# Two streams or two equal halves: how layer one's 768 tokens are cut into two matmul ranges

## The chip, the cores and the metric

The kernel runs on one core of a Trainium2 chip. The metric is the time of one execution in device microseconds (us). The kernel before took 2801.38 us, the median of three runs (2800.25 to 2804.05).

## The reference, cut to what matters

Two layers of a transformer with parallel branches run over two streams: 512 latent tokens `x` and 256 context tokens `ctx`, both 1024 wide. In each layer the input is normalised and modulated and then projected; grouped-query attention, differential attention and a convolution branch work side by side, are merged with gates, and a SwiGLU feed-forward follows. All of it is in 32-bit floats.

```python
for l in range(DEPTH):                       # DEPTH = 2
    last = l == DEPTH - 1
    h  = modulate(rms_norm(x,  g_norm1[l]), sh1,  sc1)
    hc = modulate(rms_norm(xc, g_norm1[l]), csh1, csc1)
    gq, gk, gv, dq, dk, dv, cu       = project_heads(h  @ w_in[l], *qk_gains, rope)
    gqc, gkc, gvc, dqc, dkc, dvc, cuc = project_heads(hc @ w_in[l], *qk_gains, None)
    # latent queries attend to [context keys ; latent keys], context queries to context keys
    y = merge_branches(h, o_gqa, o_diff, cu, lam_init, *branch_w)
    x = x + gt1 * y
    x = x + gt2 * swiglu(modulate(rms_norm(x, g_norm2[l]), sh2, sc2), w_ffn_in[l], w_ffn_out[l])
    if not last:
        ...                                  # the same for xc, with its own modulation
return x
```

Layer one (index 0 in the code) therefore works on all 768 tokens. In layer two (index 1) the context is only needed for keys and values, and all else works on the 512 latent tokens.

## The kernel before, in words

Activations lie transposed in SBUF, features on the 128 partitions and tokens along the free axis: columns 0 to 511 are the latent tokens, 512 to 767 the context. `H` (normalised input) and `RB` (branch results, or in attention the tiles `QB`, `KB`, `VB`, `PT`) hold each value as a high and a low part. Weights come as tiles of 128 output features by up to 1024 inputs, that is up to eight chunks of 128x128. A tile's way is: DMA from SP into one of two `STG` buffers, high part by ScalarE (ACT, L748, `hi`), low part by GpSimd (POOL, L390, `split`) into one of three slots of `WHI` and `WLO`, then TensorE (PE). `product` (L467) issues three matmuls a chunk (L469, L470, L471): high by high, high by low, low by high.

`ranges(l, wide)` (L204) says into which column ranges the tokens are cut, since one PSUM bank takes at most 512 columns. Everything that projects takes its ranges from it. `tile` (L477) runs through all chunks for the first range into one of the two banks `acc0` and `acc1`, and then through all chunks again for the second range into the other bank. With `ready`, each chunk of the first range waits until its moving data is there (after a norm, at the start of a branch, of the output projection and of the feed-forward's second half). `between` puts a small piece of other PE work into the middle of the second range (`turn_mod`, L535, the transposes of a row of the modulation, or the sums of head norms).

In attention (`attention` on PE, L607) the order is written out. A head has six items of 128 queries in layer one: four of latent queries with 768 keys and two of context queries with 256 keys. PE does for each item the transposes of the probabilities (`turn_probs`, L587), the scores of the next item (`scores`, L574), a portion of the next head's projections (`slot(j, 2*i)`), the weighted sum (`weigh`, L593), and a second portion. `FILL` (L37) gives the size of each of the twelve portions in chunks of three matmuls: `[3, 3, 2, 3, 3, 2, 3, 3, 2, 3, 2, 3]` for a grouped-query head (tiles q and a, two ranges each, 32 chunks) and `[8, 4, 4, 8, 4, 4, 8, 4, 4, 8, 4, 4]` for a differential one (k, q, v, g, 64 chunks). In both a first range ends with its third or first portion and the second range with the third after it or the next two. All projections within attention go to bank `acc0` (`tile_chunks`, L497), so a range can start only when ACT has emptied the range before: `evac_norm` (L769, one Identity into `XG`, one Square into `XS`), `evac_copy` (L795) or `evac_conv_a` (L804). These stand in ACT's own written-out order behind the softmax work of the item. DVE reduces, divides and combines the probabilities (L1169, L1189, L1202).

A range that crosses column 512 holds tokens of both streams. `stream_pieces` (L123) cuts it, and the residual (L1315), `evac_conv_a` and the convolution's splits issue one instruction a piece.

Of the kernel before, what the change touches and what calls it, by code (L numbers as in the profile page):

```python
# [30 lines left out]
LAT, CTX = 512, 256  # L31
# [98 lines left out]
def build(nc, xT, vecs, consts, wdw, w_mod, w_in, w_gate, w_br, w_out, w_fi, w_fo, out):  # L130
    x_next = nc.dram_tensor("x_next", (P, KC, LAT), F32).ap()

    with ExitStack() as ctx:
# [69 lines left out]

        def ranges(l, wide):  # L204
            if l == 0:
                return [(0, 384), (384, 384)]
            return [(0, LAT), (LAT, CTX)] if wide else [(0, LAT)]

        def blocks(l):
# [6 lines left out]
        def halves(n):  # L216
            return [(0, n // 2), (n // 2, n // 2)]

        nr = lambda l: len(ranges(l, False))
        nb = lambda l: len(blocks(l))  # L220
        kind_of = lambda j: "gqa" if j < 4 else "diff"
# [6 lines left out]
        def next_tiles(l, j):  # L228

            wide, slim = ranges(l, True), ranges(l, False)  # L230
            return ([("q", slim), ("a", slim)] if j < 4 else
                    [("k", wide), ("q", slim), ("v", wide), ("g", slim)])
# [195 lines left out]
        def _(pe):  # L428
# [240 lines left out]
            for l in range(DEPTH):  # L669
                norm(l, 0, TOK)  # L670
                wide, slim = ranges(l, True), ranges(l, False)
                n = n_tok(l)
                uses = lambda t, rngs: [at[(l, 0, t), r] for r in range(len(rngs))]
# [890 lines left out]
```

## Time and profile before

| | |
|---|---|
| median of three runs | 2801.38 us (2800.25 to 2804.05) |
| profiled execution, its own time | 2799.78 us |
| its span | 2798.0 us, 34383 instructions |
| mean granted clock of PE over the span | 0.948 of full |
| PE busy | 2478.2 us, 89% |
| DVE, ACT, POOL busy | 43%, 42%, 38% |
| attention of layer one | about 140 to 595 us |
| gated merge of layer one with the convolution | about 597 to 1010 us |
| feed-forward of layer one | about 1095 to 1694 us |
| layer two | from about 1704 us |

Times of the trace count from the start of the span. Idle time of PE stands in square brackets behind a row, with the instruction that ended it. In the listing by line "128x384" is partitions by columns. The granted clock is the share of full speed (2.4 GHz) at which PE was let run; 0.5 is the lower of its two levels, 1.2 GHz.

### The profile page before, as it was taken

To read this page: it belongs to the slowest core of one execution; us is meant where nothing else is said; L and a number is where in the kernel's file an instruction comes from. 1 tells how busy PE (TensorE), PEld (TensorE's weight loads), DVE (VectorE), ACT (ScalarE), POOL (GpSimd) and SP (SyncE) were. 2 spreads that over 40 slices of the span, in tenths; PEclk is the share of its full clock that TensorE was granted. 3 is DMA by queue.
4 is the path that set the end of the run, shared out by engine and by line. 5 is a ranking of instruction groups with operands and counts; after the bars stand their busy time and mean duration, and the time that the engine had idled before them with its cause. 6 is when DMAs were issued, how large, how long until landed. Compare 5 with 4: busy or idle time off the path is not lost.

```text
span 2798.0 us, 34383 instructions
## 1 busy us (share of the span) xinstructions
PE 2478.2 (89%) x13556; PEld 2221.6 (79%) x13556; DVE 1208.8 (43%) x1815; ACT 1169.4 (42%) x2288; POOL 1057.1 (38%) x803
## 2 busy tenths in 40 slices
PE   4788988869996998999999998888877879899998
PEld 3677877759986987999999996776766657688887
DVE  1466555568896223111111125665457982311111
ACT  3555566653334334331331225656564233422322
POOL 6311111127884542553553232111113535444443
PEclk7799999979998998999999998999988989999999
DMA  5100001003332431331332212111101213233332
GB/s 183 61 24 24 31 31 31 27 27 121 117 114 71 128 135 46 107 119 61 115 112 68 68 53 81 33 31 38 38 23 46 87 49 128 79 99 94 99 97 91
DMA packets 62062, 209.03 MB, mean 75 GB/s; under 512 B 7504, under 2 KB 7632, under 8 KB 61648
## 3 DMA queue, kind: packets, MB, share of 16 engines
q1 hardware_dynamic: 61904, 206.84, 23.6%
q8 instruction: 109, 1.79, 0.3%
q14 instruction: 49, 0.40, 0.0%
HBM read 202.62 MB, written 4.19 MB: 74 GB/s over the span
## 4 chain that ended last, share of the span: by engine, by line
PE 45%; DVE 10%; ACT 5%; issue 1%; ACTq 0%; DVEq 0%
PE acc L469 14%; PE acc L471 14%; PE acc L470 14%; DVE X L1403 5%; ACT M L752 2%; DVE M L1126 2%; DVE RB L1126 1%; PE sco L526 1%; ACT H L752 1%; PE aux L587 1%; ACT WHI L748 1%; DVE NM L1169 1%; ACT RB L752 1%; PE sco L574 0%; ACT R L752 0%
## 5 line engine op out<-in xcount | busy, mean ns | idle before, releaser
L390 POOL TENSOR_TENSOR WLO<-STG,WHI 128x512 fp32r<-128x512 f32 (+2 forms) x792 | 1053.0, 1356 | 1714.9 <-ACT WHI L748 1714.9
L469 PE MATMUL acc<-H,WHI 128*128 128x384 f32 (+2 forms) x2528 | 923.4, 365 | 94.8 <-ACT M L752 44.0
L470 PE MATMUL acc<-H,WHI 128*128 128x384 f32 (+2 forms) x2528 | 903.6, 357 | 0.0
L471 PE MATMUL acc<-H,WLO 128*128 128x384 f32 (+2 forms) x2528 | 903.1, 357 | 0.0
L748 ACT ACTIVATE WHI<-STG 128x512 fp32r<-128x512 f32 (+2 forms) x792 | 428.7, 592 | 650.4 <-PE acc L471 405.7
L469 PEld LDWEIGHTS acc<-H,WHI 128*128 128x128 f32 x2528 | 487.8, 193 | 158.1 <-issue 64.7
L471 PEld LDWEIGHTS acc<-H,WLO 128*128 128x128 f32 x2528 | 488.2, 193 | 33.7
L470 PEld LDWEIGHTS acc<-H,WHI 128*128 128x128 f32 x2528 | 489.4, 194 | 30.6
L1403 DVE SCALAR_TENSOR_TENSOR X<-U,WDW,X 128x783 f32<-128x783 f32 (+1 forms) x256 | 331.3, 1294 | 14.8 <-ACT X L752 6.9
L469 PE MATMUL acc<-RB,WHI 128*128 128x384 f32 (+1 forms) x816 | 294.6, 361 | 21.9 <-DVE T L1126 11.2
L470 PE MATMUL acc<-RB,WHI 128*128 128x384 f32 (+1 forms) x816 | 289.6, 355 | 0.0
L471 PE MATMUL acc<-RB,WLO 128*128 128x384 f32 (+1 forms) x816 | 289.5, 355 | 0.0
L1126 DVE TENSOR_TENSOR RB<-aux,RB 128x384 fp32r<-128x384 f32 (+1 forms) x236 | 118.8, 538 | 222.8 <-ACT RB L752 221.7
L1126 DVE TENSOR_TENSOR T<-G,acc 128x384 f32<-128x384 f32 (+1 forms) x114 | 68.3, 599 | 324.6 <-PE acc L471 319.7
L1315 DVE SCALAR_TENSOR_TENSOR X<-acc,MOD,X 128x384 f32<-128x384 f32 (+1 forms) x128 | 67.6, 549 | 322.9 <-PE acc L471 322.9
L469 PEld LDWEIGHTS acc<-RB,WHI 128*128 128x128 f32 x816 | 154.4, 189 | 40.7 <-DVE T L1126 14.2
L752 ACT ACTIVATE M<-sco,NM 128x768 f32<-128x768 f32 (+1 forms) x160 | 129.8, 814 | 84.3 <-DVE NM L1169 84.3
L471 PEld LDWEIGHTS acc<-RB,WLO 128*128 128x128 f32 x816 | 154.5, 189 | 10.8
L470 PEld LDWEIGHTS acc<-RB,WHI 128*128 128x128 f32 x816 | 154.5, 189 | 10.1
L1126 DVE TENSOR_TENSOR MOD<-sco,V 128x4 f32<-128x4 f32 x48 | 7.8, 162 | 356.8 <-PE sco L543 356.5
L587 PE MATMUL aux<-K,M 128*128 128x128 f32 x624 | 98.0, 289 | 68.2 <-DVE M L1202 30.5
L587 PEld LDWEIGHTS aux<-K,M 128*128 128x128 f32 x624 | 73.2, 146 | 90.8 <-issue 44.9
(106 smaller groups left out, 2493.2 us busy)
## 6 DMA issues: line engine op xcount, KB each, us to landing
STG<-in_w_mod SPq DMA_DIRECT2D x96, 512.0 KB, 3.5
STG<-in_w_fi SPq DMA_DIRECT2D x88, 512.0 KB, 3.5
STG<-in_w_in SPq DMA_DIRECT2D x52, 512.0 KB, 3.5
STG<-in_w_gate SPq DMA_DIRECT2D x48, 512.0 KB, 3.5
STG<-in_w_fo SPq DMA_DIRECT2D x32, 512.0 KB, 3.5
STG<-in_w_br SPq DMA_DIRECT2D x48, 256.0 KB, 2.5
STG<-in_w_out SPq DMA_DIRECT2D x16, 512.0 KB, 3.6
X<-in_xT SPq DMA_DIRECT2D x2, 3072.0 KB, 11.7
```

Source lines behind the costliest of these rows:

```text
L390: nc.gpsimd.tensor_tensor(WLO[:, s, a:a + w], STG[:, g, a:a + w], WHI[:, s, a:a + w].bitcast(F32), ALU.subtract).then_inc(S("w_split"), 1)
L469: nc.tensor.matmul(dst, lh, rh, start=first, stop=False)
L470: nc.tensor.matmul(dst, lh, rl, start=False, stop=False)
L471: return nc.tensor.matmul(dst, ll, rh, start=False, stop=last)
L526: mm = nc.tensor.matmul(sco[0][:, 0:MOD_GROUP], SCX[:, 4 * (4 * q + k):4 * (4 * q + k) + P], w[:, s, k * MOD_GROUP:(k + 1) * MOD_GROUP], s ...
L587: t = nc.tensor.transpose(dst[:, n * P:(n + 1) * P], PR[:, slot, (k - k0) * P:(k - k0 + 1) * P], IDENT)
L748: nc.scalar.activation(WHI[:, s, a:a + w], STG[:, g, a:a + w], ACT.Copy).then_inc(S("w_hi"), 1)
L752: ins = nc.scalar.activation(dst, src, f, **kw)
L1126: return nc.vector.tensor_tensor(dst, a, b, op)
L1169: nc.vector.tensor_reduce(NM[:, slot:slot + 1], sco[m][:, 0:n], AX_X, ALU.max, negate=True).then_inc(S(f"max{m}"), 1)
L1315: nc.vector.scalar_tensor_tensor(X[:, j, s:s + m], acc[b][:, s - a:s - a + m], MOD[:, l, part, j, st:st + 1], X[:, j, s:s + m], ALU.mult, ...
L1403: own("tap", nc.vector.scalar_tensor_tensor(o, u, wt, o, ALU.mult, ALU.add))
```

## The change

In layer one the two ranges of every weight tile are now 512 and 256 columns, the latent tokens and the context tokens, in place of 384 and 384. Layer two's ranges were already cut this way. `LAT` is 512 and `CTX` is 256.

```diff
--- before.py
+++ after.py
@@ -203,7 +203,7 @@
 
         def ranges(l, wide):
             if l == 0:
-                return [(0, 384), (384, 384)]
+                return [(0, LAT), (LAT, CTX)]
             return [(0, LAT), (LAT, CTX)] if wide else [(0, LAT)]
```

What it moves can't be seen in that line. PE, first item of the seventh head of layer one: the end of the first range of tile k, the sums of squares of the head before (L605), and the start of the second range. Before:

```order
L469 MATMUL acc0<-H,WHI 128x384
L470 MATMUL acc0<-H,WHI 128x384
L471 MATMUL acc0<-H,WLO 128x384
L605 MATMUL aux1<-T,K 128x256
L469 MATMUL acc0<-H,WHI 128x384
L470 MATMUL acc0<-H,WHI 128x384
L471 MATMUL acc0<-H,WLO 128x384
```

Now:

```order
L469 MATMUL acc0<-H,WHI 128x512
L470 MATMUL acc0<-H,WHI 128x512
L471 MATMUL acc0<-H,WLO 128x512
L605 MATMUL aux1<-T,K 128x256
L469 MATMUL acc0<-H,WHI 128x256
L470 MATMUL acc0<-H,WHI 128x256
L471 MATMUL acc0<-H,WLO 128x256
```

No instruction of PE changes its place; the portion of eight chunks is wider and the portions of four chunks behind it are narrower.

ACT, the same place: the last copy of tile g of the head before, its sigmoid between two table loads, a weight tile, the softmax work, and the evacuation of tile k's first range (the last two rows). Before:

```order
L752 ACTIVATE M<-acc0 128x384
L752 ACT_TABLE_LOAD
L752 ACTIVATE M<-M 128x768
L758 ACT_TABLE_LOAD
L748 ACTIVATE WHI<-STG 128x512 x2
L752 ACTIVATE RB<-aux1 128x3x128
L752 ACTIVATE RB<-aux0 128x3x128
L752 ACTIVATE M,L<-sco0,NM 128x768
L752 ACTIVATE M,L<-sco1,NM 128x768
L752 ACTIVATE M<-M,RLN 128x768
L752 ACTIVATE M<-acc0,EC,V 128x384
L752 ACTIVATE M<-acc0 128x384
```

Now:

```order
L752 ACTIVATE M<-acc0 128x256
L752 ACT_TABLE_LOAD
L752 ACTIVATE M<-M 128x768
L758 ACT_TABLE_LOAD
L748 ACTIVATE WHI<-STG 128x512 x2
L752 ACTIVATE RB<-aux1 128x3x128
L752 ACTIVATE RB<-aux0 128x3x128
L752 ACTIVATE M,L<-sco0,NM 128x768
L752 ACTIVATE M,L<-sco1,NM 128x768
L752 ACTIVATE M<-M,RLN 128x768
L752 ACTIVATE M<-acc0,EC,V 128x512
L752 ACTIVATE M<-acc0 128x512
```

The order is the same, the copy ahead is narrower and the evacuation wider.

DVE, the residual behind the output projection, two output tiles. Before:

```order
L1315 SCALAR_TENSOR_TENSOR X<-acc0,MOD,X 128x384
L1315 SCALAR_TENSOR_TENSOR X<-acc1,MOD,X 128x128
L1315 SCALAR_TENSOR_TENSOR X<-acc1,MOD,X 128x256
L1315 SCALAR_TENSOR_TENSOR X<-acc0,MOD,X 128x384
L1315 SCALAR_TENSOR_TENSOR X<-acc1,MOD,X 128x128
L1315 SCALAR_TENSOR_TENSOR X<-acc1,MOD,X 128x256
```

Now:

```order
L1315 SCALAR_TENSOR_TENSOR X<-acc0,MOD,X 128x512
L1315 SCALAR_TENSOR_TENSOR X<-acc1,MOD,X 128x256
L1315 SCALAR_TENSOR_TENSOR X<-acc0,MOD,X 128x512
L1315 SCALAR_TENSOR_TENSOR X<-acc1,MOD,X 128x256
```

A tile takes two instructions instead of three, since no range crosses from one stream to the other.

## Rows read from the trace of the kernel before

**Rows 1.** The page, busy time of each engine, share of the span, instructions.

```profile
PE 2478.2 (89%) x13556; PEld 2221.6 (79%) x13556; DVE 1208.8 (43%) x1815; ACT 1169.4 (42%) x2288; POOL 1057.1 (38%) x803
```

**Rows 2.** Windows, PE alone, in layer one's feed-forward: stretch, length, busy, clock, DMA.

```profile
1120.00:1260.00 140.00, 140.00 (x841) 1.00 0.37 113
```

**Rows 3.** Timeline, PE: start, duration, engine, line, operation, operands, width.

```profile
204.39 0.28 PE L470 MATMUL acc<-RB 128*128 128x256 f32 x1
...
206.30 0.28 PE L471 MATMUL acc<-RB 128*128 128x256 f32 x1
...
640.05 0.34 PE L469 MATMUL acc<-H,WHI 128*128 128x384 f32 x1
...
648.20 0.34 PE L471 MATMUL acc<-H,WLO 128*128 128x384 f32 x1
...
2649.93 0.39 PE L469 MATMUL acc<-RB,WHI 128*128 128x512 f32 x1
...
2657.87 0.39 PE L471 MATMUL acc<-RB,WLO 128*128 128x512 f32 x1
```

**Rows 4.** Timeline, PE, heads six (to 485) and seven of layer one.

```profile
456.46 0.88 PE L587 MATMUL aux<-K,M 128*128 128x128 f32 x6 [0.89 <-DVE M L1202]
...
472.42 0.44 PE L469 MATMUL acc<-H,WHI 128*128 128x384 f32 x1 [1.09 <-ACT M L752]
...
478.49 0.41 PE L587 MATMUL aux<-K,M 128*128 128x128 f32 x2 [0.99 <-DVE RB L1126]
...
485.51 0.87 PE L587 MATMUL aux<-K,M 128*128 128x128 f32 x6 [0.30 <-DVE M L1202]
...
497.01 0.66 PE L469 MATMUL acc<-H,WHI 128*128 128x384 f32 x1 [4.60 <-ACT M L752]
```

**Rows 5.** Groups by line and form, ACT: count, busy us, mean ns, idle before.

```profile
L752 ACT ACTIVATE M<-acc 128x384 f32<-128x384 f32 x44 | 21.2, 481 | 17.6 <-PE acc L471 17.6
L752 ACT ACTIVATE M<-acc,EC,V 128x384 f32<-128x384 f32 x26 | 17.2, 663 | 27.0 <-PE acc L471 27.0
...
L752 ACT ACTIVATE M<-acc 128x512 f32<-128x512 f32 x22 | 13.0, 590 | 13.1 <-PE acc L471 8.5 <-DVE RB L1126 4.7
L752 ACT ACTIVATE M<-acc,EC,V 128x512 f32<-128x512 f32 x13 | 10.1, 773 | 18.6 <-PE acc L471 18.5
L752 ACT ACTIVATE M<-acc 128x256 f32<-128x256 f32 x10 | 3.8, 379 | 14.0 <-PE acc L471 14.0
L752 ACT ACTIVATE M<-acc,EC,V 128x256 f32<-128x256 f32 x5 | 2.8, 564 | 17.4 <-PE acc L471 17.4
```

**Rows 6.** Windows, all engines: PE, PEld, DVE, ACT, POOL busy, clock, DMA.

```profile
431.00:437.00 6.00, 5.55 (x31) 5.11 (x31) 1.88 (x4) 1.96 (x5) 0.00 (x0) 0.72 0.00 0
497.00:503.00 6.00, 5.99 (x22) 5.53 (x24) 1.04 (x2) 1.63 (x4) 0.00 (x0) 0.53 0.01 3
```

**Rows 7.** Timeline, PE, layer two, after waits for an evacuation.

```profile
1982.93 0.36 PE L469 MATMUL acc<-H,WHI 128*128 128x256 f32 x1 [3.87 <-ACT M L752]
...
2012.49 0.58 PE L469 MATMUL acc<-H,WHI 128*128 128x256 f32 x1 [3.37 <-ACT M L752]
```

**Rows 8.** Timeline, ACT, evacuations of the first tile of layer one.

```profile
105.00 0.67 ACT L752 ACTIVATE M<-acc,EC,V 128x384 f32<-128x384 f32 x1 [1.43 <-PE acc L471]
...
110.03 0.67 ACT L752 ACTIVATE M<-acc,EC,V 128x384 f32<-128x384 f32 x1 [3.98 <-PE acc L471]
```

**Rows 9.** Ends of stages: timeline of DVE and PE, and a DVE group by form.

```profile
1006.93 0.44 PE L469 MATMUL acc<-RB,WHI 128*128 128x384 f32 x1 [1.91 <-ACT G L752]
...
1083.95 0.74 DVE L1315 SCALAR_TENSOR_TENSOR X<-acc,MOD,X 128x128 f32<-128x128 f32 x2 [3.48 <-PE acc L471]
...
L1315 DVE SCALAR_TENSOR_TENSOR X<-acc,MOD,X 128x256 f32<-128x256 f32 x32 | 15.2, 475 | 0.0
```

**Rows 10.** Timeline, PE, a grouped-query head of layer one.

```profile
219.55 1.51 PE L587 MATMUL aux<-K,M 128*128 128x128 f32 x6 [2.04 <-DVE RB L1126]
```

**Rows 11.** Waits of PE from 620 to 860 us, in the merge: total us, times, longest.

```profile
PE sco L543 <- ACT R L752: 15.1, 15, 1.6
```

## The prediction

> **What bounds the kernel now.** I read the busy shares first: TensorE (PE) is busy for 89% of the span [rows 1], so its work and its idle time set the end. Then the feed-forward part of layer one in windows: 140 us with no idle time at all and the granted clock at full level, 1.00 (2.4 GHz) [rows 2]. There only the time from one matmul to the next counts. Next the timeline of single matmuls for that time at each width [rows 3], then the timeline of the second half of attention, where PE waits for ScalarE (ACT) and VectorE (DVE) between portions of projection [rows 4]. So the change has two faces: a price per pair of matmuls, and a new rhythm where projections fill the gaps of attention.
>
> **Price of a pair.** Each weight chunk is used by a 384 and a 384 before, by a 512 and a 256 now; instructions on PE and columns stay the same. From 640.05 to 648.20 lie 47 starts of 384 columns: 0.1734 us each. From 2649.93 to 2657.87, 35 of 512: 0.2269. From 204.39 to 206.30, 16 of 256: 0.1194 [rows 3]. A pair costs 0.3468 before and 0.3463 after. Layer one multiplies 26x24 (input projection), 24x24 (gates), 24x12 (branches), 8x24 (output), 44x24 and 22x24 (feed-forward) such pairs, 3264 in all. 3264 x -0.5 ns = **-1.6 us**, with an end at each side of 3 us because starts are written to 0.01 us.
> The Trainium skill (TensorE: Matmul & The Clock Gate, Back-to-back issue gap) gives columns/2.4 GHz + 2.5 ns for an isolated warm gap, by which an estimate of both pairs is 325 ns and the term would be 0. The rows show the three spacings 10 to 12 ns above that formula at every width, so the difference stays near 0 by either.
>
> **Where the first range is fed chunk by chunk.** At the start of layer one and of its feed-forward, PE runs its first range at the pace at which ACT and DVE deliver H, chunk by chunk, and at the low clock. Before, the second range takes 110.03 - 105.00 = 5.03 us [rows 8]; 24 x 0.1734 is 4.16, so 0.87 us are lost to the low level (1.2 GHz), which is 1.7 us of it. Now the first range still ends with the feed, plus 0.3 us for three wider last matmuls; the second has 24 x 0.1194 = 2.87 us plus 0.7 lost. Gain 5.03 - 0.3 - 3.55 = 1.2 us, twice: **-2.3 us**.
>
> **Ends of stages.** The residual crosses from tokens to context inside its second range and takes two DVE instructions, 0.74 us together; 256 columns alone take 0.475 [rows 9]. -0.26 us, twice. The branch tile at 1006.93 waits 1.91 us with its second range for the sigmoid [rows 9]; that range now starts 12 x 0.0535 = 0.64 us later, and that much of the wait is filled. Together **-1.2 us**. In the gated merge PE waits 15.1 us in 15 turns of the modulation row [rows 11]. The turn stands before the last six matmuls of a tile's second range; they take 0.72 instead of 1.04 us. Where the weight pipeline (DMA, ACT, POOL) sets the round nothing comes of this, where PE's gate tile restarts it, 0.3 us per round or per two: between 0 and -5, I take **-1.0 us**, nearer to none because all 15 rounds wait, so the pipeline sets most of them.
>
> **The filler in attention.** Its portions are counted in chunks, not in columns. A tile of the differential heads is handed out as 8 chunks (the whole first range), then 4 and 4 (the second). 8 chunks were 4.16 us and become 5.44 (+1.28); 4 were 2.08 and become 1.43 (-0.65). The six query tiles of a head get: +1.28-0.65, -0.65+1.28, -1.30, +1.28-0.65, -0.65+1.28, -1.30. Summed this is zero, but a portion that shrinks ahead of a wait saves nothing. Head seven, from 485.51, item by item [rows 4]:
> First item: the second portion waits 4.60 us, until ACT has emptied the bank (497.01). ACT's chain begins with the last copy of the head before. PE's last portion now ends earlier, so the copy starts earlier too; I take 0.3 us, as long as PE itself waits at 485.51; and it is 0.1 shorter (0.379 against 0.481) [rows 5]; emptying takes 0.773+0.590 instead of 0.663+0.481, +0.22. The portion starts 0.2 us earlier after a wait of 4.60-1.28-0.2 = 3.1 us, and is 0.65 shorter: -0.8. Second: the wide portion starts when ACT has emptied a 256 bank (-0.20), lasts +1.28, and the transposes behind it wait for a 512 evacuation (+0.22): +1.3. Third: at 456.46 in the head before PE already waits 0.89 us for DVE's probabilities, a chain that PE's portions do not touch; the saved 1.30 becomes waiting, 2.2 us: 0. Fourth: no wait, +0.6. Fifth: at 472.42 PE waits 1.09 for ACT; the short portion before it saves only 0.1, the wide one costs 1.28, and the copy at 478.49 0.1: +1.3. Sixth: PE already waits 0.30 for the probabilities at 485.51: 0. Sum **+2.4 us a head, three heads; the last grouped-query head, which fills for the first differential one, is nearly the same (+3.0)**; the head without filler starts 0.4 earlier. Together **+9.8 us**. In the three heads before, portions are 2 or 3 chunks and the same walk gives +1.0 and -1.0 in turn, with waits for evacuations that shift by 0.2: 0, ends -3 and +3.
>
> **The clock behind the long wait.** After 4.60 us of waiting the granted clock is low: 0.72 and 0.53 over six microseconds in two heads [rows 6], that is 3.4 and 5.6 us at half speed, which cost 1.7 and 2.8 us; 2.25 on average, 6.8 for three heads. The wait becomes 3.1 us. Layer two has waits of the same kind: after 3.87 us a 256 matmul still took 0.36 (full level), after 3.37 us one took 0.58 (low) [rows 7]. So it can go either way; I take two of three dips as gone, **-4.5 us**. Against that the third item's wait grows to 2.2 us; one wait of 2.04 was followed by a slow stretch, 1.51 us for transposes that take 0.88 elsewhere [rows 10, 4]: **+1.3 us**. The Trainium skill says in the same page (Part 1) that an idle PE falls back to the half clock and that sustained activity releases it; by it alone the dips' share of the sum would be anything from 0 to -6.8. These rows show both outcomes.
>
> Sum against the profiled execution's 2799.8: -1.6 -2.3 -1.2 -1.0 +9.8 -4.5 +1.3 = +0.5, so 2800.3; the median of the runs lies 1.6 us above that execution, so 2802 us.
>
> **Rivals.** (a) Slower: the clock. All three dips stay (+4.5) and the new waits of 2.2 and 1.6 us, six in number, bring dips of their own in half of the cases, some 2 us each (+6 more): about 2812 us. It decides where the granted clock behind 3.1 us of waiting is still near 0.6. For it: the wait of 3.37 and that of 2.04 that were followed by the low level. Against: most short waits were not.
> (b) Faster: the waits follow. If the probability chains start earlier because evacuations of 256 columns leave ACT's queue sooner, the third and sixth items save what I count as waiting, up to 1.3 us each in four heads; half of it gives -5, and with all dips gone -2, so about 2794 us. Against it: at 456.46 the wait ends with a DVE instruction whose chain begins at PE's own transposes.
> (c) The weight load becomes the limit of a 256 matmul. Loads have records of their own, 2221.6 us for 13556 of them, 0.164 each [rows 1], longer than 0.119. If they could not overlap, 3264 x 0.045 = +147 us, about 2948 us. The sixteen starts at 0.119 speak against it: they too have a load of 128 columns each, from `RB`.
> (d) The change does nothing that can be seen, because both faces are within a microsecond: 2801.4 us. The new order of rows excludes that the program is unchanged.
>
> **How the numbers follow.** A measurement of this kernel tells about 0.2% from no change, 5.6 us: from 2795.8 to 2807.0. My forecast, 0.48, has its own range of 2796 to 2808 by the ends of the terms (3 us for the pair, 3 for the short portions, 4 for the merge, 2 to 4 for the clock); rival (d) 0.07, (a) 0.24, (b) 0.19, (c) 0.02. All of (d), 0.46 of the forecast and a little of (a) and (b) give same 0.57, faster 0.19, slower 0.24. The range of 8 in 10 reaches to the middle of both neighbours: 2793 to 2812.
>
> **What would show it.** The pair at 0.346 us and windows of the feed-forward without idle time; the wait for ACT before the second portion of a differential head at about 3.1 us; waits of about 2.2 and 1.6 us for DVE's probabilities in the third and sixth items; a differential head longer by 2.4 us at the same clock; the second range at layer start 3.6 us after the first. It is wrong if the heads keep their length, if a 256 matmul follows another by more than 0.125 us, or if the granted clock falls in places with no long wait.

## The result and the profile after

| | before | after |
|---|---|---|
| median, 15 runs each | 2800.31 us (2796.74 to 2806.17) | 2806.28 us (2801.77 to 2811.06) |
| profiled execution, own time | 2799.78 us | 2801.77 us |
| its span and granted clock | 2798.0 us, 0.948 | 2800.0 us, 0.951 |

The ratio of the medians is 1.002, with a 95% interval of 1.0012 to 1.0027: a small loss, 6.0 us, at the edge of the 0.2% that counted as no change. The range held it (2793 to 2812). The profiled execution of after is the fastest of its 15, so its trace shows a loss of only 2.0 us; what a more usual execution looks like is shown further down by a second profile of the same kernel.

The busy line of the page of after answers to [rows 1]:

```profile
PE 2477.8 (88%) x13556; PEld 2093.5 (75%) x13556; DVE 1208.5 (43%) x1783; ACT 1171.8 (42%) x2284; POOL 1056.6 (38%) x803
```

TensorE's busy time is the same to 0.4 us. DVE has 32 instructions fewer (the residuals), ACT four. The loss, then, is time in which PE waits, not work added to it.

The feed-forward of layer one, PE alone (stretch, length, busy, clock, DMA share, GB/s), answers to [rows 2]:

```profile
1120.00:1260.00 140.00, 140.00 (x844) 1.00 0.37 113
```

It is full as before. From its first turn of the modulation row to its last (1123.74 to 1474.62 before, 1123.46 to 1474.48 after) it takes 350.88 and 351.02 us. The pair of widths costs nothing and gives nothing.

The timeline of PE in the differential heads six and seven of layer one answers to [rows 4]. "In the third item" means behind that item's portions, ahead of the transposes of the next. These are all the rows from 441 to 501 us behind a wait of over 1 us, with four of those that follow the longest wait for probabilities:

```profile
441.38 0.50 PE L469 MATMUL acc<-H,WHI 128*128 128x512 f32 x1 [1.27 <-ACT M L752]
...
457.07 0.87 PE L587 MATMUL aux<-K,M 128*128 128x128 f32 x6 [2.22 <-DVE M L1202]
457.87 0.67 PE L574 MATMUL sco<-RB 64*128 64x256 f32 x6
458.47 0.80 PE L469 MATMUL acc<-H,WHI 128*128 128x512 f32 x1
459.06 0.63 PE L470 MATMUL acc<-H,WHI 128*128 128x512 f32 x1
...
462.38 0.39 PE L470 MATMUL acc<-H,WHI 128*128 128x512 f32 x1
...
475.10 0.50 PE L469 MATMUL acc<-H,WHI 128*128 128x512 f32 x1 [1.64 <-ACT M L752]
...
482.59 0.41 PE L587 MATMUL aux<-K,M 128*128 128x128 f32 x2 [1.10 <-DVE RB L1126]
...
489.62 0.88 PE L587 MATMUL aux<-K,M 128*128 128x128 f32 x6 [1.58 <-DVE M L1202]
...
500.81 0.36 PE L469 MATMUL acc<-H,WHI 128*128 128x256 f32 x1 [2.96 <-ACT M L752]
```

Read it against the walk of the prediction. Before the second portion PE waits 2.96 us where it waited 4.60 (3.1 forecast). In the third item it waits 2.22 for the probabilities (0.89 before, 2.2 forecast), in the sixth 1.58 (0.30 before, 1.6 forecast). The two wide portions, in the second and the fifth item, start after waits of 1.27 and 1.64. So every wait came out where it was expected, within 0.2 us. What did not come is the clock: the matmul behind the 2.96 us runs at full level (0.36 us), but behind the 2.22 us the clock falls, and 512 columns take 0.63 us where they take 0.39 a little later.

The waits of PE grouped by what ended them (total us, times, longest), over three differential heads of before:

```profile
PE acc L469 <- ACT M L752: 19.8, 9, 4.9
PE aux L587 <- DVE M L1202: 4.0, 7, 0.9
```

and of after:

```profile
PE acc L469 <- ACT M L752: 18.1, 9, 3.5
PE aux L587 <- DVE M L1202: 13.2, 7, 2.2
```

1.7 us less for ScalarE's evacuations, 9.2 more for VectorE's probabilities (1.3 of them at the end of head four, ahead of head five's first transposes). From the first transposes of head five to those of head eight, 353.84 to 552.35, that is 198.51 us before; after, 353.43 to 557.67, it is 204.24: **+5.7 us**, the largest piece of the change. The next is head four, which fills for the first differential head: 287.44 to 353.84 before, 283.94 to 353.43 after, +3.1 us.

The other pieces have the other sign. Rows of after for the ends of stages answer to [rows 9]: the branch tile's second range, the statistics of the feed-forward's norm, and the first fed chunk behind them.

```profile
1009.81 0.39 PE L469 MATMUL acc<-RB,WHI 128*128 128x256 f32 x1 [1.09 <-ACT G L752]
...
1088.43 1.64 PE L656 MATMUL acc<-M,K 128*128 128x384 f32 x4 [2.52 <-DVE M L1126]
...
1096.04 0.76 PE L469 MATMUL acc<-H,WHI 128*128 128x512 f32 x1 [4.26 <-DVE H L1126]
```

Before, these rows stand at 1006.93 with a wait of 1.91, at 1086.69 with 2.78, and at 1095.59 with 4.90. The wait of 2.52 is 0.26 shorter, the 0.26 us that the forecast had for the residual that no longer crosses the two streams. From the last turn of layer one's merge to the first of its feed-forward (1008.39 to 1123.74 before, 1011.20 to 1123.46 after) the stage is 3.1 us shorter.

Along the whole program the lead of after over before, in us (minus is earlier): first transposes of attention -2.4, head five -0.4, head eight +5.3, first turn of the merge +5.3, gate tiles done +3.7, output projection +2.8, feed-forward -0.3, its last turn -0.1, end +2.0. The last 2 us come in layer two, whose rows are the same in both kernels; from the sums of its first norm to the end it is 2.5 us longer here than before, and in the seven other traces between 1.5 us shorter and 5.4 us longer, so no part of this is put down to the change.

### The profile page after: what moved, and what is told of

Its sections match the earlier page's. It is cut to its first block, busy times and chain, and to the rows that moved or that the text cites. A ratio compares the mean times of both kernels' runs of the same rounds, so it can differ in the third digit from the quotient of the medians.

```text
span 2800.0 us, 34347 instructions
## 1 busy us (share of the span) xinstructions
PE 2477.8 (88%) x13556; PEld 2093.5 (75%) x13556; DVE 1208.5 (43%) x1783; ACT 1171.8 (42%) x2284; POOL 1056.6 (38%) x803
## 4 chain that ended last, share of the span: by engine, by line
PE 61%; DVE 14%; ACT 12%; DMA 5%; POOL 5%; issue 2%; SPq 0%; ACTq 0%; DVEq 0%
PE acc L469 19%; PE acc L471 18%; PE acc L470 18%; ACT M L752 6%; DVE X L1403 5%; POOL WLO L390 5%; DMA STG<-in_w_mod 5%; DVE RB L1126 3%; ACT WHI L748 2%; PE aux L587 2%; DVE M L1126 2%; PE sco L574 2%; DVE NM L1169 2%; PE sco L526 2%; ACT RB L752 1%
## 5 line engine op out<-in xcount | busy, mean ns | idle before, releaser
L469 PE MATMUL acc<-H,WHI 128*128 128x512 f32 (+1 forms) x2528 | 924.3, 366 | 90.2 <-ACT M L752 43.5
L470 PE MATMUL acc<-H,WHI 128*128 128x512 f32 (+1 forms) x2528 | 905.0, 358 | 0.0
L471 PE MATMUL acc<-H,WLO 128*128 128x512 f32 (+1 forms) x2528 | 903.9, 358 | 0.0
L469 PEld LDWEIGHTS acc<-H,WHI 128*128 128x128 f32 x2528 | 488.1, 193 | 187.1 <-issue 59.9
L471 PEld LDWEIGHTS acc<-H,WLO 128*128 128x128 f32 x2528 | 488.9, 193 | 68.1
L469 PE MATMUL acc<-RB,WHI 128*128 128x512 f32 (+1 forms) x816 | 295.1, 362 | 20.2 <-DVE T L1126 11.2
L470 PE MATMUL acc<-RB,WHI 128*128 128x512 f32 (+1 forms) x816 | 290.4, 356 | 0.0
L471 PE MATMUL acc<-RB,WLO 128*128 128x512 f32 (+1 forms) x816 | 289.9, 355 | 0.0
L1126 DVE TENSOR_TENSOR RB<-aux,RB 128x384 fp32r<-128x384 f32 (+1 forms) x236 | 119.0, 538 | 222.0 <-ACT RB L752 220.8
L1126 DVE TENSOR_TENSOR T<-G,acc 128x512 f32<-128x512 f32 x114 | 68.1, 597 | 320.6 <-PE acc L471 315.8
L1315 DVE SCALAR_TENSOR_TENSOR X<-acc,MOD,X 128x512 f32<-128x512 f32 x96 | 63.5, 661 | 323.6 <-PE acc L471 323.6
L469 PEld LDWEIGHTS acc<-RB,WHI 128*128 128x128 f32 x816 | 155.0, 190 | 50.0 <-DVE T L1126 14.1
L471 PEld LDWEIGHTS acc<-RB,WLO 128*128 128x128 f32 x816 | 154.8, 190 | 22.3
L587 PE MATMUL aux<-K,M 128*128 128x128 f32 x624 | 99.7, 293 | 78.5 <-DVE M L1202 40.2
L752 ACT ACTIVATE M<-sco,NM 128x768 f32<-128x768 f32 (+1 forms) x160 | 129.9, 815 | 86.5 <-DVE NM L1169 86.5
L1126 DVE TENSOR_TENSOR MOD<-sco,V 128x4 f32<-128x4 f32 x48 | 7.8, 162 | 361.2 <-PE sco L543 360.8
L587 PEld LDWEIGHTS aux<-K,M 128*128 128x128 f32 x624 | 73.4, 148 | 100.2 <-issue 46.3
```

Source lines behind the costliest of these rows:

```text
L469: nc.tensor.matmul(dst, lh, rh, start=first, stop=False)
L470: nc.tensor.matmul(dst, lh, rl, start=False, stop=False)
L471: return nc.tensor.matmul(dst, ll, rh, start=False, stop=last)
L587: t = nc.tensor.transpose(dst[:, n * P:(n + 1) * P], PR[:, slot, (k - k0) * P:(k - k0 + 1) * P], IDENT)
L752: ins = nc.scalar.activation(dst, src, f, **kw)
L1126: return nc.vector.tensor_tensor(dst, a, b, op)
```

## Experiments

Each was run beside the kernel before, on the same chip. The first four were on one chip, where the kernel before had a median of 2804.02 us (23 runs), the last three on another, where it had 2802.15 (29 runs); times are compared with the one beside them. Where an edit adds two lines ahead of it, L469 to L471 read L471 to L473, L587 L589, L605 L607, L752 L754, L1126 L1128, and L1202 L1204. The trace of before is the one of the first profile throughout. (`FILL` stands at L47 of the kernel.)

### e1_attn384: equal halves in attention, two streams elsewhere

```diff
             wide, slim = ranges(l, True), ranges(l, False)
+            if l == 0:
+                wide = slim = [(0, 384), (384, 384)]
```

on the changed kernel.

> Ranges of 512 and 256 everywhere in layer one but in attention's portions (heads two to eight), which go back to 384 and 384. Filler theory: the changed kernel's profile gains 2.4 us ahead of attention, about 2 in the merge and 3.5 between merge and feed-forward, and loses 7.7 within attention; without that loss the kernel is at 2792 to 2795 us, faster than before (2800), and the first weighted sums of heads show no wait of 2.2 us for DVE's probabilities. Pair theory (a 256 matmul costs more than half a 512 one, everywhere): attention holds 504 of 3264 pairs, so at most a sixth of the loss goes and it stays at 2805.

Measured: 2799.93 us (2791.33 to 2807.72, 12 runs), ratio 0.9988 (0.9976 to 0.9999). The waits of the differential heads are those of before, and at the feed-forward's start this kernel is 4.0 us earlier than before and stays so. The loss is gone and a small gain has taken its place: 4.1 us by the medians, where 2792 to 2795 against 2800 was 5 to 8. (By `FILL` the portions hold 528 of the 3264 pairs, not 504; a sixth either way.) The pair theory, which left the loss at five sixths, is excluded. In this trace the stage of the gate tiles is 1.8 us longer than before, where after has 1.6 less; which of its waits makes that was not followed up. One row bears on the clock: behind a wait of 4.55 us a matmul of 384 columns still started at the full level, where the same form took 0.66 us behind 4.60 before, and 0.6 us later the granted clock fell.

```profile
497.79 0.41 PE L471 MATMUL acc<-H,WHI 128*128 128x384 f32 x1 [4.55 <-ACT M L754]
```

### e2_onlyattn: two streams in attention alone

The same edit on the kernel before, with `[(0, LAT), (LAT, CTX)]` in place of the halves.

> The complement: 384 and 384 everywhere in layer one, 512 and 256 only in attention's portions. Filler theory: 2807 to 2810 us, slower than before by the whole 7 to 10 us, differential heads of 68 us instead of 66. Pair theory: 2801 us.

Measured: 2812.70 us (2808.78 to 2815.36, 5 runs), ratio 1.003 (1.0018 to 1.0042). At the merge's first turn its trace is 9.4 us later than before, 8.7 of it since attention's first transposes, with the waits of after:

```profile
436.85 0.36 PE L471 MATMUL acc<-H,WHI 128*128 128x256 f32 x1 [2.98 <-ACT M L754]
...
461.14 0.88 PE L589 MATMUL aux<-K,M 128*128 128x128 f32 x6 [2.21 <-DVE M L1204]
...
493.71 0.88 PE L589 MATMUL aux<-K,M 128*128 128x128 f32 x6 [1.59 <-DVE M L1204]
```

Together the two halves of the change give -4.1 and +8.7 us by their medians against 2804.02, +4.6 in sum, where the whole change gave 6.0. Both signs are those of the filler theory, and the second size too (7 to 10 us); the pair theory had neither. So the change splits: the loss is made in attention, a gain outside of it.

### e3_fill538: other portions for the wide and narrow ranges

```diff
-    (0, "diff"): [8, 4, 4, 8, 4, 4, 8, 4, 4, 8, 4, 4],
+    (0, "diff"): [5, 3, 8, 5, 3, 8, 5, 3, 8, 5, 3, 8],
```

on the changed kernel: the wide range is handed out as 5 and 3 chunks, the narrow one as 8.

> The changed kernel with the portions of the differential heads cut 5, 3, 8 instead of 8, 4, 4: 3.4, 2.0 and 2.9 us, so that the third and the sixth item get 4.9 us and not 2.9. Filler theory: the waits of 2.2 and 1.6 us for the probabilities fall under 0.5, each of three heads is shorter by 3.5 to 4.5 us, the clock dip behind the third item goes, and the kernel is at 2793 to 2796 us. If the loss were in the evacuations or the pair, it would stay within 2 us of the changed kernel's 2806.

Measured: 2808.64 us (2804.94 to 2814.29, 11 runs), ratio 1.0018 (1.0008 to 1.0027): a miss. The timeline of PE in head six shows why:

```profile
437.39 0.87 PE L587 MATMUL aux<-K,M 128*128 128x128 f32 x6 [2.83 <-DVE M L1202]
...
459.28 0.58 PE L469 MATMUL acc<-H,WHI 128*128 128x256 f32 x1 [3.09 <-ACT M L752]
...
490.71 0.38 PE L469 MATMUL acc<-H,WHI 128*128 128x256 f32 x1 [1.84 <-ACT M L752]
```

The waits for probabilities in the third and sixth items are gone, as meant. But the first item's portions are now so short that PE waits 2.83 us for probabilities behind them, and in the third and sixth items it waits 3.09 and 1.84 us for the bank. A range that ends in the first portion of an item is evacuated by ACT behind that item's softmax work, so the range that follows it has to start an item later or wait. The head is 68.2 us long (437.39 to 505.56), as in after, although PE waits only 9.9 us in it instead of 11.4. The rest is the clock: two stretches at the low level fall into head six (3.4 us each, from 438.50 and 458.98), where after has one. So the waits that this layout adds stand in for most of those that it removes, and the dips, which were to go, take what is left. The portions were laid out by their length alone; where a range ends mattered as much.

### e4_ctxfirst: the same two ranges in the other order

```diff
-                return [(0, LAT), (LAT, CTX)]
+                return [(LAT, CTX), (0, LAT)]
```

for layer one, everywhere.

> The changed kernel with the context range first (256, then 512 columns) everywhere in layer one. Filler theory: portions become 2.9, 2.7, 2.7 us, every item gets 5.4 to 5.6 us, the waits of third and sixth items nearly go and attention gains 8 to 10 us; against that the tile fed chunk by chunk ends with 24 matmuls of 512 instead of 256, +2.6 us at two places, +0.3 at two residual tails, and the turn in the merge has 0.6 us more behind it, up to +5 in 16 rounds. In sum 2800 to 2806 us. Pair theory: no change from 2806 but for the fed tiles, 2811.

Measured: 2812.76 us (2807.41 to 2815.52, 5 runs), ratio 1.0032 (1.0019 to 1.0045). A miss in sum, but the best test of two terms. First, the order of ranges where the moving data is fed chunk by chunk: the stage from the merge's last turn to the feed-forward's first, 3.1 us shorter in after, is here 118.4 us against 115.35, 3.0 longer. With the narrow range first, most of the columns come after the feed. The first tile alone shows it, from its first chunk to the start of the next tile: 20.68 us before, 18.09 after and 22.01 here at the start of the layer; 21.80, 20.44 and 22.79 in the feed-forward; 10.80, 10.64 and 13.45 in the output projection. So the gain does come from what is left to do once the last chunk has arrived, and it turns its sign with the order; the output projection gains nearly nothing from the wide range first and loses most from the narrow one. Second, the differential heads: the portions are now narrow, wide, wide, and no wait for probabilities is left in them. PE in heads six and seven:

```profile
435.02 0.77 PE L469 MATMUL acc<-H,WHI 128*128 128x512 f32 x1 [4.65 <-ACT M L752]
...
475.48 0.39 PE L469 MATMUL acc<-H,WHI 128*128 128x256 f32 x1 [0.52 <-ACT M L752]
...
499.97 0.77 PE L469 MATMUL acc<-H,WHI 128*128 128x512 f32 x1 [4.65 <-ACT M L752]
```

From 435.02 to 499.97 a head takes 64.95 us: 3.1 less than in after, about what its waits have less (8.1 against 11.4 us), and less than before too (65.6 to 66.8), although the long wait is back at 4.65 us and the clock is low behind it (0.77 us for 512 columns). Other stages still make the sum a loss: by 387 us the trace is 4.5 us behind before, and from 1475 to 2120 us it falls back by some 6 us more, with a clock of 0.93 against 0.95 from 1700 to 1950.

### e7_mixed: each stage with the cut that suits it

```diff
             wide, slim = ranges(l, True), ranges(l, False)
+            if l == 0:
+                wide = slim = [(0, 384), (384, 384)] if j < 4 else [(LAT, CTX), (0, LAT)]
```

on the changed kernel: latent first outside of attention, equal halves in the grouped-query heads, context first in what fills the differential heads.

> The changed kernel, but what fills the grouped-query heads of layer one is cut 384/384, and what fills the differential heads is cut into the 256 context columns first and the 512 latent columns second. Theory A (the fill's portions decide in attention, the cut outside of it gains about 4 us by the end of the output projection): the waits for probabilities before the third and sixth item's transposes stay under 1 us, the differential heads are about 65 us each (before 66.1, 65.6, 66.8), attention's end is about 4 us earlier than before, the feed-forward's start about 8 us earlier, the median 2795 to 2798, 0.997 to 0.998 of before. Rival B (the shorter differential heads of the context-first kernel only made up for what it had lost further ahead): differential heads as before within 0.3 us each, the median as with 384/384 in attention, 2800 (0.999). Rival C (the clock: the wait before the second portion of the first item, 4.6 us with the context first, lowers the clock for longer, as in the context-first kernel, which had 0.87 to 0.91 there): slower heads, 2803 or more.

Measured: 2795.87 us (2792.57 to 2803.25, 12 runs), ratio 0.9981 (0.997 to 0.9992), and 11.7 us less than the changed kernel on the same chip (e9_after_again). Theory A holds. The profiled execution is the fastest of its twelve (2792.57 us), so its stages flatter the kernel by some 3 us. The waits of PE over the three differential heads:

```profile
PE acc L471 <- ACT M L754: 18.9, 11, 6.7
PE aux L607 <- DVE RB L1128: 6.3, 3, 3.4
PE aux L589 <- DVE RB L1128: 2.8, 3, 0.9
PE aux L589 <- ACT R L754: 0.6, 3, 0.2
```

There is no row for the probabilities any more (13.2 us in after, 4.0 before). The row for L607 is a new wait: 1.4 us ahead of the norm sums in heads six and seven, and 3.4 at the start of head eight, where before has 2.8. In head six alone PE waits 8.0 us, 9.1 before and 11.4 after. The two rows of the timeline that mark a head,

```profile
429.25 0.76 PE L471 MATMUL acc<-H,WHI 128*128 128x512 f32 x1 [4.65 <-ACT M L754]
...
494.15 0.76 PE L471 MATMUL acc<-H,WHI 128*128 128x512 f32 x1 [4.65 <-ACT M L754]
```

are 64.9 us apart. Attention ends 4.4 us earlier than before, the feed-forward begins 9.8 earlier, the end is 7.2 earlier in the profiled pair.

Rival C was right about the dips, all three of which stand behind the 4.65 or 6.74 us (PE, PEld, DVE, ACT, POOL busy, clock, DMA):

```profile
429.00:439.00 10.00, 9.75 (x46) 7.89 (x47) 4.05 (x8) 3.63 (x9) 0.00 (x0) 0.82 0.00 0
494.00:504.00 10.00, 9.85 (x47) 7.97 (x48) 3.98 (x8) 3.60 (x10) 0.00 (x0) 0.82 0.01 2
440.00:485.00 45.00, 42.83 (x270) 35.23 (x269) 25.87 (x45) 30.26 (x65) 8.45 (x6) 1.00 0.12 36
```

but wrong about their weight: 10 us at 0.82 lose 1.8, and before has dips behind the same wait too; the rest of the head, at 1.00, wins more. Rival B is excluded: the three heads take 65.0, 64.9 and 64.9 us against 66.1, 65.6 and 66.8.

### e8_diffctx: context first in the differential heads, nothing else

The edit of e7_mixed on the kernel before.

> The kernel before, with 384/384 everywhere but in what fills the differential heads of layer one, which is cut into 256 context columns and then 512 latent columns. Theory A: the three differential heads are shorter by 1 us each, the rest as before: about 0.9988 of before, 2800 to 2801. Rival B: 1.000, differential heads as before. Rival C (the clock behind the wait of 4.6 us): 1.001 or more.

Measured: 2800.46 us (2796.75 to 2803.09, 12 runs), ratio 0.9989 (0.998 to 0.9999), as theory A had it. From the first norm sums (L605) of head five to those of head seven, 387.29 to 519.67 before, it is 132.38 us; here, 390.15 to 519.92, 129.77: 1.3 a head. Over all three heads it is 3.8 us. It had lost 2.9 us by 390. Of these 2.0 stand already at the context items of the last grouped-query head (348.50 against 346.50), whose own projections are cut as before; the clock from 142 to 300 us is 0.97 against 0.98. By attention's end it is even with before in the trace.

### e9_after_again: the changed kernel a second time

> The changed kernel once more, on the chip and beside the runs of the two others. If the loss of the changed kernel is its own and not that of one chip or one placement: 1.001 to 1.003 of before, 6 us, and the profile again without a dip of the clock behind the waits of about 3 us in the first items of the differential heads, but with one behind the waits of 2.2 us in their third items. If the clock behind such waits is chance: other waits show the dips this time.

Measured: 2807.61 us (2802.89 to 2813.43, 12 runs), ratio 1.002 (1.001 to 1.0031), as the first time. Its profiled span is 2806.7 us, near its median. The waits repeat to 0.02 us (3.47, 2.94 and 2.95 before the second portions, 2.22, 2.22 and 2.20 in the third items). The dips do not. The windows behind these waits in heads six and seven, first after:

```profile
432.00:443.00 11.00, 8.96 (x67) 8.11 (x68) 6.51 (x12) 7.41 (x17) 1.08 (x1) 1.00 0.00 0
457.00:468.00 11.00, 10.93 (x50) 8.66 (x51) 6.49 (x15) 6.58 (x16) 2.52 (x2) 0.84 0.16 48
500.00:511.00 11.00, 8.92 (x67) 8.07 (x68) 6.51 (x12) 7.45 (x17) 1.03 (x1) 1.00 0.01 1
525.00:536.00 11.00, 10.88 (x49) 8.64 (x50) 6.53 (x15) 6.57 (x16) 2.52 (x2) 0.84 0.16 49
```

then the same program again:

```profile
436.00:447.00 11.00, 9.47 (x62) 8.48 (x63) 5.08 (x11) 6.04 (x14) 0.02 (x1) 0.84 0.00 0
461.50:472.50 11.00, 10.38 (x58) 8.56 (x59) 7.35 (x16) 7.73 (x17) 2.55 (x2) 1.00 0.17 48
504.00:515.00 11.00, 9.42 (x62) 8.45 (x63) 5.07 (x11) 6.04 (x14) 0.00 (x0) 0.84 0.01 1
529.50:540.50 11.00, 10.33 (x58) 8.53 (x59) 7.35 (x16) 7.78 (x17) 2.55 (x2) 1.00 0.17 49
```

In one execution the dip stands behind the third item's wait, in the other behind the first item's; one in each of these heads, 0.84 over 11 us, either way. In head five both have it behind the first item's wait of 3.46 and 3.47 us, 0.84 and 0.74 over 11 us. So it isn't the length of the one wait that decides it.

## Why the prediction held, and where it did not

The time lies inside the range and 4 us above the forecast of 2802; in attention the forecast's mechanism, wait by wait, is what happened. That the total comes near is in part luck: several terms are off by 1 to 2 us, with both signs, and stages that the two kernels share moved by as much. Term by term, in the profiled pair:

| term | forecast | measured |
|---|---|---|
| pair of widths | -1.6 | about 0 |
| first range fed chunk by chunk | -2.3 | -3.4 |
| ends of stages | -1.2 | -0.8, and -2.1 more in the same stage |
| merge turns | -1.0 | -1.6 |
| filler in attention | +9.8 | +10.2, and -1.1 in heads one to three |
| clock in the heads (-4.5 + 1.3) | -3.2 | -1.4 (-0.4 in the second profile) |
| layer two and the rest | 0 | about +2 |

**Pair.** Between starts a 512 took 0.2283 us (24 from 1164.06 to 1169.54) and a 256 0.1192 (13 from 1169.54 to 1171.09): 0.3475 against 0.3468 before. The -0.5 ns of the prediction is no more than the rounding of its rows, as its own end of 3 us allowed. Estimates by the page of the Trainium skill that it cited (TensorE: Matmul & The Clock Gate, Back-to-back issue gap) gave zero for this term, which is what the feed-forward shows (350.88 and 351.02 us); the spacings themselves are again above that formula, by 10 to 13 ns.

**Feed.** From the first fed chunk to attention's first transposes it took 53.28 us before and 50.65 after, -2.6; in the feed-forward to its first turn 28.15 and 27.42, -0.7. The forecast had 1.2 for each. The sum is 1.1 better; at the start of the layer the clock stood at 1.00 from the last fed chunk on, where before it was 0.96 over the stretch to attention. ScalarE takes up the second range 2.8 us behind the first there (107.69 and 104.87), where the forecast's sign was 3.6, since no low level was left in it. The other traces put this in its place: the first of these stretches takes 53.2 to 54.6 us in the three with equal halves there, and 50.7 to 52.6 in the five with the wide range first. That is 2.0 on average, so some 0.6 of the 2.6 may be chance. In the feed-forward the averages differ by the same 0.7.

**Ends.** The round with the sigmoid's wait (991.19 to 1008.39, 994.56 to 1011.20) is 0.56 us shorter, and the residual's wait 0.26, against 0.64 and 0.26. What the stage gained beyond that, about 2 us, the prediction did not have. Of this 1.3 is clock, which the cut does not fix: the four matmuls of the statistics took 2.93 us before and 1.64 after, with the same columns, and in e8_diffctx, whose cut is that of before in this stage, 1.56. From the last turn of the merge to the first of the feed-forward the three traces with equal halves have 115.4, 114.4 and 113.7 us, the five with the wide range first 111.9 to 113.2: 2.1 less on average, not 3.1.

**Merge.** The turns' waits fell from 15.1 [rows 11] to 12.8 us, and the stage by 1.6. This gain is not shown to be the change's: from its first turn to its sixteenth it takes 237.0 to 237.3 us in the three traces with equal halves and 235.7 to 239.0 in the five with 512 and 256.

**Filler.** The three differential heads are 5.7 us longer together. PE waits 27.6 us in them before and 34.7 after, behind each head's first transposes up to those of the next: +7.1, or 2.4 a head, the forecast's number. PE's busy time in them fell by 1.3 us (170.85 to 169.54), which is the clock's part. The last grouped-query head is 3.1 us longer, at full clock in both, where the forecast had 3.0. Together +10.2, as forecast (9.8 with the -0.4 of the head that has no filler, which changed by 0.0). The first three grouped-query heads, for which the forecast had 0, are 1.1 shorter; they have two stretches of 3.4 us at the low level before (from 171.59 and 219.37) and one after (from 140.87).

**The term that was mis-sized** is the one on the clock behind the long wait: "I take two of three dips as gone, -4.5 us". The wait did fall to 3 us, but each of the three heads kept a dip: in head five at the old place, shorter, in heads six and seven behind the third item's wait. The stretches in which PE runs at the low level, before:

```profile
365.22:369.56 4.34, 4.34 (x14) 0.50 0.00 0
431.45:434.41 2.96, 2.96 (x9) 0.50 0.00 0
497.01:502.68 5.67, 5.67 (x20) 0.50 0.01 3
```

and after:

```profile
366.15:369.56 3.41, 3.41 (x20) 0.50 0.00 0
458.31:461.72 3.41, 3.41 (x12) 0.50 0.00 0
526.57:529.98 3.41, 3.41 (x9) 0.50 0.02 5
```

Half of these 12.97 and 10.23 us is lost, 6.5 and 5.1: a gain of 1.4 us where the forecast's two terms had 3.2. In the second profile of after they are 5.38, 3.41 and 3.41 us, a gain of only 0.4. Attention as a whole (from its first transposes to the merge) cost 7.7 us in the first profile, 9.5 in the second and 8.7 in e2_onlyattn. The forecast had 6.6. These 1 to 3 us are part of the distance from the forecast to the median. The rest is not in one place: the second profile is also 1.7 us behind the first between the gate tiles and the branches, at a clock of 0.90 against 0.95 from 870 to 1010 us, in rows that the two share.

**The rivals.** (a), slower by the clock, did not come: in heads six and seven new dips took the place of the old ones but were not added to them, and the median is 6 us below its 2812. (b), waits that follow, is excluded by the 2.22 and 1.58. (c) is excluded by the 0.119 between 256-column matmuls, although a weight load's own record lasts 0.19 us there (the 0.164 of the prediction divides busy time, in which overlapping loads count once): the loads do overlap. (d), nothing to be seen, is excluded too: the interval of the ratio lies above 1 in both sets of runs of the changed kernel, and its two halves have effects of opposite sign.

## What to carry to other kernels

A cut of the free axis that costs nothing per matmul still decides two things: how much work is left when a fed operand's last chunk arrives (the first tile of the feed-forward took 21.8 us with equal halves, 20.4 with the wide range first, 22.8 with the narrow one first), and how long each piece of filler is between waits. Where filler is counted in chunks, write the length of every portion in microseconds next to the wait that ends behind it; time taken from a portion ahead of a wait turns into waiting, time added to a portion ahead of none is paid in full. And look at where a range ends, since its evacuation stands in another engine's queue. The cut need not be the same in all stages: e7_mixed uses three and is 0.9981 of before. And compare more than one trace of a kernel before a difference of 1 or 2 us in a stage is given to the change: stages that two kernels share differed by that much here.

## What the runs showed of the hardware that was not expected

The waits of the same program repeat to 0.02 us from one execution to the next, but the place of the low clock does not: behind the 2.2 us wait in one, with 1.00 behind the 3.0 us wait, and the other way round in the next. Behind a wait of 3.46 or 3.47 us the next 256-column matmul took 0.36 us in one execution and 0.55 in two others; in the first of these the clock fell 1.5 us later all the same. Behind 4.55 to 4.91 us a 384-column matmul took 0.66 us in five cases (three before, two in e1_attn384) and 0.41 in one, with the fall 0.6 us later. Behind 4.65 and more, the 512-column matmul took 0.76 or 0.77 us in all nine cases (three each in e4_ctxfirst, e7_mixed and e8_diffctx). What in the engine's work before decides between the two levels at the shorter waits stays open.
